# A causal attention stage: value products of two units together, the side products dealt anew, part of q copied by transfers

## The chip, the cores and the metric

The kernel runs on one NeuronCore of a Trainium2 chip. The metric is the device time of one execution in microseconds (us). TensorE (PE) does the matrix products, VectorE (DVE), ScalarE (ACT) and GpSimd (POOL) do the element-wise work, and SyncE (SP) issues most of the DMA transfers. Each engine works through its own instruction stream strictly in the order of the program, and the streams meet only at semaphores: an instruction `wait_ge(s, n)` holds its engine until the counter s has reached n.

## What is computed

One decoder layer on 1024 tokens of width 1024: a pooling mixer and a causal attention with a forget bias side by side, gated and projected; then a cross attention to 256 memory tokens; then a SwiGLU feed-forward layer and a last RMSNorm. The change lies in the causal attention (8 heads of width 64) and in the pooling mixer's output product that runs beside it:

```python
for i in range(S // Q_BLOCK):                       # 8 blocks of 128 queries
    q0, q1 = i * Q_BLOCK, (i + 1) * Q_BLOCK
    s = jnp.einsum('bhqd,bhkd->bhqk', q[:, :, q0:q1], k[:, :, :q1]) * scale
    s = s + c[:, :, q0:q1, None] - c[:, :, None, :q1]   # forget bias
    s = jnp.where(mask[None, None], s, -1e30)
    p = jax.nn.softmax(s, axis=-1)
    outs.append(jnp.einsum('bhqk,bhkd->bhqd', p, v[:, :, :q1]))
y_pool = pool_mixer(u_pool, pool_w, pool_scale) @ w_pool_out
gates = jax.nn.sigmoid(g_logit + b_gate)            # g_pool, g_fox
x = x + (g_pool * y_pool + g_fox * y_fox) @ w_out
```

## The kernel before

The attention is a loop over 32 units, written out once for each engine. Unit u treats the pair of heads p = u // 8 and the query block i = u % 8, so a unit has i + 1 blocks of 128 keys for each of two heads. It is a pipeline over three units:

- PE, scores of unit u (lines 2396 to 2413): two float32r products per head and per 512 keys, into PSUM banks 0 to 3. They wait for `sc_biased` of unit u - 1, because DVE must have read the same banks.
- DVE (lines 1767 to 1777) adds the bias `negc`, finds the minimum (the negated maximum) and writes `prob`. ACT takes the exponential (line 1242), DVE multiplies by the reciprocal of the sum (lines 1785 and 1787) and counts `prob_ready`.
- PE, one unit later: transposes of `prob` (line 2384) in groups of up to four blocks into banks 4 and 5 in turn; ACT copies each group to `prob_t` (line 1233). From the third group on a group waits for the copy that frees its bank.
- PE, two units later: value products `values(u - 2)` (line 2375) into bank 6, with weights of 64 columns, so the array works in two halves of 64 columns. ACT copies the result to `o_sb` (`pv_copy`, line 1215).

So unit u on PE is, in this order: scores(u), values(u - 2), first two groups of transposes(u - 1), side work part 0, the other groups of transposes, side work part 1. In units with i = 0 part 0 stands before the values and part 1 before the later transposes.

Side work (`fill`, line 2327) fills PE's waiting time: the last four products of the stage before (d), eight mixing products (m), and from the twelfth unit on 64 pieces, four for each of 16 output halves v of the pooling mixer's projection. A piece is three products of 512 columns (`mm3`, lines 2172 to 2174), here called a piece. All 16 halves use the same PSUM bank, 7: the first piece of half v waits for `za_done >= v` (line 2356), that is, until DVE has multiplied half v - 1 out of the bank with its gate (`pool_gated`, line 1758). The tables FIRST_FILL and NEXT_FILL (lines 148 to 150) say how many pieces each part of each unit gets, two numbers for a unit. GATED_IN (line 156) derives from them the part in which a half's last piece lies, and DVE's stream has its multiply in that unit: if it is part 0 with i of 4 or more (or 0), behind DVE's bias step of the unit; if it is part 0 with i of 1 to 3, or part 1, behind DVE's multiplies by the reciprocal.

ACT's order in a unit is: the value copy, the copies of the first two groups, the two exponentials, the copies of the other groups, then side jobs. Among these are the splits of the next pair's q and k into a high and a low part (`qk_hi_of`, line 1106). For q each head's scaled half (64 partitions) is written twice by ACT, once into its own partitions and once into the other 64 (lines 1112 and 1114). When a pair is complete, its result is split too (`o_hi_of` on ACT, `o_lo_of` on DVE; units 27 to 29 and behind the loop).

Of the kernel before, what the change touches and what calls it, by code (L numbers as in the profile page):

```python
# [15 lines left out]
FP32 = mybir.dt.float32  # L16
# [6 lines left out]
P = 128  # L23
# [63 lines left out]
LAST = (4, 5, 6, 7, 0, 1, 2, 3)  # L87
PROD2 = 7
# [60 lines left out]
NEXT_FILL = ((0, 2, 1, 1, 2, 2, 1, 2) + (1, 2, 1, 1, 2, 2, 2, 2, 2, 2, 1, 1, 1, 1, 1, 2)  # L149
             + (1, 4, 2, 2, 2, 2, 2, 2, 2, 2, 1, 1, 1, 1, 1, 3))  # L150
# [70 lines left out]
def build(nc, x, mem, norm_mix_g, w_in, b_forget, b_gate, pool_w, pool_scale, w_pool_out,  # L221
# [15 lines left out]
    with ctx:  # L237
# [76 lines left out]
        prob_t = place("prob_t", 136, [P, 2, S])  # L314
        o_sb = place("o_sb", 144, [P, PAIRS, S])
# [90 lines left out]
        pads_zero, win_step, d_ready, d_stored = (sem("pads_zero"), sem("win_step"), sem("d_ready"),  # L406
# [10 lines left out]
        negc_masked, negc_plain = sem("negc_masked"), sem("negc_plain")  # L417
        qk_hi, qk_lo, q2_zeroed, negc_loaded = sem("qk_hi"), sem("qk_lo"), sem("q2_zeroed"), [sem(f"negc_loaded{i}") for i in range(3)]
# [6 lines left out]
        mem_loaded, gain_row_in, ones_set, gain_spread, mix_gain = (sem("mem_loaded"), sem("gain_row_in"), sem("ones_set"),  # L425
# [141 lines left out]
        def _(sp):  # L567
# [88 lines left out]
            def load_qk(p, r):  # L656

                which, h = divmod(r, 2)
                i = r % 2
                if (p, r) in ((2, 0), (2, 1)):  # L660
                    sp.wait_ge(prod_done, N_STAGE + 3)
                if p > 1 or r >= 2:
                    sp.wait_ge(qk_lo, 8 * p + 2 * r - 2 if r >= 2 else 8 * p - 4 + 2 * r + 2)
                else:
                    for s in range(4):
                        sp.wait_ge(c_stored[s], 16 * FST[s, QK_REST[1]])
                    sp.wait_ge(prod_done, N_STAGE)
                sp.dma_start((qk_first if p == 1 else qk_st)[:, i, :], qk_dram[3 * which + p - 1][:, half_of(h)]).then_inc(qk_in[i], 16)
# [388 lines left out]
        def _(act):  # L1057
# [48 lines left out]
            def qk_hi_of(p, r, src, a0=0, a1=2):  # L1106

                which, h = divmod(r, 2)
                for a in range(a0, a1):
                    own, other = slice(a * DH, (a + 1) * DH), slice((1 - a) * DH, (2 - a) * DH)  # L1110
                    if which == 0:
                        nc.scalar.activation(q1[p % 2][a][other, half_of(h)], src[own, :], ACT.Copy,
                                             scale=DH ** -0.5).then_inc(qk_hi, 1)
                    nc.scalar.activation((k1 if which else q1)[p % 2][a][own, half_of(h)], src[own, :], ACT.Copy,
                                         scale=1.0 if which else DH ** -0.5).then_inc(qk_hi, 1)
# [94 lines left out]
            def pv_copy(v):  # L1210
                act.wait_ge(pv_done, v + 1)
                if v == 2 * T:
                    for s in range(4):
                        act.wait_ge(c_stored[s], 16 * FST[s, LAST_PAIR])
                nc.scalar.activation(o_sb[:, v // T, tile_of(v % T)], ps[:, 6, 0:P], ACT.Copy).then_inc(pv_copied, 1)
# [6 lines left out]
            for u in range(PAIRS * T + 1):  # L1222
# [3 lines left out]
                if u >= 2:  # L1226
                    pv_copy(u - 2)
                groups = list(enumerate(groups_of((u - 1) % T))) if u else []

                def copy_groups(part):  # L1230
                    for g, (a, j0, n) in part:
                        act.wait_ge(pt_done, groups_before(u - 1) + g + 1)
                        nc.scalar.activation(prob_t[:, a, j0 * P:(j0 + n) * P], ps[:, 4 + g % 2, 0:n * P],  # L1233
# [23 lines left out]
                if u in (27, 28, 29):  # L1257
                    o_hi_of(u - 27)
# [223 lines left out]
        def _(dve):  # L1482
# [24 lines left out]
            nc.vector.memset(ones_row[:], 1.0).then_inc(ones_set, 1)  # L1507
            dve.wait_ge(consts_set, 6)
            nc.vector.tensor_copy(count[:], count_i[:]).then_inc(pads_zero, 1)
            dve.wait_ge(pads_zero, 1)  # L1510
            nc.vector.reciprocal(inv_count[:], count[:]).then_inc(pads_zero, 1)
# [181 lines left out]
            for n, (g, q) in enumerate(STAGE):  # L1693
                if (g, q) == (U_PAIRS[0], P1):
                    dve.wait_ge(negc_stored, 16)
                    nc.vector.memset(u_sb[:, :, 0:PAD], 0.0).then_inc(pads_zero, 1)
                    for w in win:
                        nc.vector.memset(w[:, 0:PAD], 0.0).then_inc(pads_zero, 1)
                    dve.wait_ge(pads_zero, 5)
# [64 lines left out]
            for u in range(PAIRS * T + 1):  # L1764
# [39 lines left out]
                if u in (27, 28, 29):  # L1804
                    o_lo_of(u - 27)
# [362 lines left out]
        def _(pe):  # L2168
# [88 lines left out]
            pe.wait_ge(ones_set, 1)  # L2257
# [134 lines left out]
            for u in range(PAIRS * T + 1):  # L2392
# [370 lines left out]
```

## Time and profile before

| | us |
|---|---|
| median of 3 runs | 1449.02 (1448.48 to 1449.16) |
| the profiled execution | 1448.73 |
| its span, first to last instruction | 1446.9 |
| PE busy in it | 1421.5 |
| DVE busy | 977.0 |
| ACT busy | 626.9 |
| POOL busy | 559.3 |

The attention runs from about 336 us to 523 us of the span. A row of a timeline gives the start, the duration, the engine, the line, the output and inputs, and how many equal instructions were merged; brackets give the idle time before it and what ended that. A product's duration runs until its last result is written, so products overlap: two of 512 columns follow each other 0.23 us apart although each lasts 0.39 us.

### The profile page before, as it was taken

What the parts mean: (1) busy time and instruction counts of PE and PEld (TensorE: products, weight loads), DVE (VectorE), ACT (ScalarE), POOL (GpSimd) and SP (SyncE); (2) the same over time, 40 slices, a digit from 0 to 9 for tenths busy, and PEclk for the clock granted to TensorE, in tenths of its full rate; (3) what the DMA queues carried; (4) which work ended last, traced back from release to release, by engine and by line L of the source; (5) the groups of instructions that cost most, each with busy time, mean ns of one, the idle gap of its engine ahead of it and who ended that gap; (6) DMA issues with size and microseconds to landing.
All of it is one profiled execution on the core that took longest, in us unless ns stands there. A gap on an engine that the chain in (4) does not pass through costs nothing.

```text
span 1446.9 us, 19339 instructions
## 1 busy us (share of the span) xinstructions
PE 1421.5 (98%) x7065; PEld 1170.8 (81%) x7065; DVE 977.0 (68%) x1393; ACT 626.9 (43%) x1181; POOL 559.3 (39%) x572
## 2 busy tenths in 40 slices
PE   7999999999999999999999999999999999999997
PEld 5778888887678788888888788888888888888886
DVE  7745595646877755327566887777677676795867
ACT  6545343526877642116543533332233222444445
POOL 5743233334555301005011755444444453354402
PEclk9999999999999999999999999999999999999999
DMA  8265263555332145114113213333233334883334
GB/s 212 60 118 124 54 146 80 80 104 181 103 102 91 50 160 203 59 44 145 31 44 117 73 59 110 109 110 109 82 108 109 110 109 183 304 291 97 93 102 146
DMA packets 104952, 166.88 MB, mean 115 GB/s; under 512 B 7278, under 2 KB 63106, under 8 KB 103451
## 3 DMA queue, kind: packets, MB, share of 16 engines
q1 hardware_dynamic: 98072, 145.55, 34.1%
q0 software_dynamic: 3200, 11.57, 2.3%
q10 hardware_dynamic: 3586, 8.52, 1.5%
q8 instruction: 57, 0.93, 0.3%
q14 instruction: 37, 0.30, 0.1%
HBM read 123.32 MB, written 42.30 MB: 114 GB/s over the span
## 4 chain that ended last, share of the span: by engine, by line
PE 89%; ACT 4%; POOL 3%; DVE 2%; issue 1%; DMA 1%; SPq 0%; DVEq 0%; ACTq 0%; POOLq 0%
PE ps L2172 27%; PE ps L2174 27%; PE ps L2173 27%; PE ps L2375 2%; PE ps L2384 2%; ACT prob L1242 1%; ACT prob_t L1233 1%; DMA raw_f<-in_w_in 1%; PE ps L2412 1%; PE ps L2411 1%; PE ps L2179 1%; PE ps L2243 1%; PE ps L2546 0%; POOL tok_f L857 0%; PE ps L2657 0%
## 5 line engine op out<-in xcount | busy, mean ns | idle before, releaser
L2172 PE MATMUL ps<-t_lo,s_hi 128*128 128x512 f32 x308 | 119.9, 389 | 0.1
L2174 PE MATMUL ps<-t_hi,s_lo 128*128 128x512 f32 x308 | 119.8, 389 | 0.0
L2173 PE MATMUL ps<-t_hi,s_hi 128*128 128x512 f32 x308 | 119.8, 389 | 0.0
L2172 PE MATMUL ps<-h_lo_T,w_hi 128*128 128x512 f32 x256 | 100.5, 392 | 1.3 <-ACT u_t L1156 1.0
L1416 ACT ACTIVATE s_hi<-w_raw 128x512 fp32r<-128x512 f32 x77 | 48.7, 632 | 118.0 <-PE ps L2174 91.7
L2174 PE MATMUL ps<-h_hi_T,w_lo 128*128 128x512 f32 x256 | 99.7, 389 | 0.0
L2173 PE MATMUL ps<-h_hi_T,w_hi 128*128 128x512 f32 x256 | 99.6, 389 | 0.0
L1501 DVE TENSOR_TENSOR s_lo<-w_raw,s_hi 128x512 fp32r<-128x512 f32 x77 | 61.1, 793 | 56.3 <-ACT s_hi L1416 56.2
L1432 ACT ACTIVATE p_sb<-ps 128x512 f32<-128x512 f32 x22 | 13.0, 598 | 189.5 <-PE ps L2174 189.5
L2172 PE MATMUL ps<-hf_lo_T,w_hi 128*128 128x512 f32 x212 | 82.5, 389 | 0.0
L2173 PE MATMUL ps<-hf_hi_T,w_hi 128*128 128x512 f32 x212 | 82.5, 389 | 0.0
L2174 PE MATMUL ps<-hf_hi_T,w_lo 128*128 128x512 f32 x212 | 82.5, 389 | 0.0
L2172 PE MATMUL ps<-h_lo_B,w_hi 128*128 128x512 f32 x192 | 76.6, 399 | 3.0 <-DVE h_lo_B L1501 3.0
L2174 PE MATMUL ps<-h_hi_B,w_lo 128*128 128x512 f32 x192 | 75.3, 392 | 0.0
L2173 PE MATMUL ps<-h_hi_B,w_hi 128*128 128x512 f32 x192 | 75.2, 392 | 0.0
L1501 DVE TENSOR_TENSOR w_lo<-s_sum,w_hi 128x512 fp32r<-128x512 f32 x64 | 48.5, 763 | 39.2 <-ACT w_hi L1104 38.8
L964 POOL TENSOR_TENSOR w_sum<-w_raw 128x512 f32<-128x512 f32 x11 | 14.3, 1296 | 156.2 <-DVE w_lo L1501 93.7
L1065 ACT ACTIVATE w_hi<-w_raw 128x1024 fp32r<-128x1024 f32 x32 | 33.9, 1059 | 89.5 <-PE ps L2174 85.9
L2172 PEld LDWEIGHTS ps<-t_lo,s_hi 128*128 128x128 f32 x308 | 57.8, 188 | 12.6 <-issue 0.5
L2174 PEld LDWEIGHTS ps<-t_hi,s_lo 128*128 128x128 f32 x308 | 57.8, 188 | 12.1
L2173 PEld LDWEIGHTS ps<-t_hi,s_hi 128*128 128x128 f32 x308 | 57.8, 188 | 11.9
L2032 DVE TENSOR_TENSOR hq<-ps,p_sb 128x512 f32<-128x512 f32 x11 | 7.6, 690 | 85.6 <-DMA hs_dram<-h_sum 64.6
(380 smaller groups left out, 4320.3 us busy)
## 6 DMA issues: line engine op xcount, KB each, us to landing
w_raw<-hs_dram SPq DMA_DIRECT2D x77, 256.0 KB, 2.7
raw_p<-in_w_ffn_in SPq DMA_DIRECT2D x22, 512.0 KB, 4.6
w_raw<-in_w_ffn_in SPq DMA_DIRECT2D x22, 512.0 KB, 4.3
hs_dram<-h_sum SPq DMA_DIRECT2D x11, 1024.0 KB, 8.9
hs_dram<-hq SPq DMA_DIRECT2D x11, 768.0 KB, 7.0
wq_B<-in_w_ffn_out SPq DMA_DIRECT2D x8, 1024.0 KB, 7.5
raw_f<-in_w_in SPq DMA_DIRECT2D x14, 512.0 KB, 7.3
gate_dram<-c_st SPq DMA_DIRECT2D x28, 256.0 KB, 2.2
```

The lines of the kernel that those rows point to most:

```text
L1065: nc.scalar.activation(w_hi[n % SLOTS][:], w_raw[n % RAWS][:], ACT.Copy).then_inc(hi_ready, 1)
L1233: nc.scalar.activation(prob_t[:, a, j0 * P:(j0 + n) * P], ps[:, 4 + g % 2, 0:n * P], ACT.Copy).then_inc(pt_copied, 1)
L1242: nc.scalar.activation(prob[u % 2][:, a, 0:n], prob[u % 2][:, a, 0:n], ACT.Exp, bias=neg_max[:, u % 2, a:a + 1], scale=-1.0, accum_out=pro ...
L1416: nc.scalar.activation(s2_hi[n % SLOTS2][:], s_raw(n % SLOTS2), ACT.Copy).then_inc(s_split_hi, 1)
L1501: nc.vector.tensor_tensor(out, a, hi.bitcast(FP32), ALU.subtract).then_inc(done, 1)
L2172: nc.tensor.matmul(dst, w_h, x_l, start=start, stop=False, skip_group_check=onto)
L2173: nc.tensor.matmul(dst, w_h, x_h, start=False, stop=False, skip_group_check=onto)
L2174: return nc.tensor.matmul(dst, w_l, x_h, start=False, stop=stop, skip_group_check=onto)
L2179: last = nc.tensor.transpose(two(bank)[:, tile_of(k)], src[:, tile_of(k)], ident[:])
L2243: last = nc.tensor.matmul(ps[0:F_ROWS + HEADS, 5 * h, :], f_w[:, KD * h + 4 * part + j, :], (h_lo if x else h_hi)[ops[part]][:, j, :], sta ...
L2375: last = nc.tensor.matmul(ps[a * DH:(a + 1) * DH, 6, 0:P], v_sb[:, j, hc:hc + DH], prob_t[:, a, tile_of(j)], start=j == 0, stop=j == v % T)
L2384: last = nc.tensor.transpose(ps[:, 4 + g % 2, tile_of(j - j0)], prob[v % 2][:, a, tile_of(j)], ident[:])
```

## The change

- PE does the value products of units 9 to 30 in pairs: none in odd units from 11 on, and in each even unit u from 12 to 32 those of u - 3 and then u - 2 (`values_in`). They use two column blocks of bank 6 in turn, and ACT's two copies stand together. The transposed probabilities of the odd units go to buffers of their own (`odd_t`), in places that others have left; ACT waits in units 10 and 30 for these to be free.
- The pieces of side work of units 12 to 31 are dealt anew (NEXT_FILL). The number of pieces in each couple of an even and the next odd unit stays the same.
- ACT writes only q's own half from the second pair on; two transfers on SP's queue for each half of the columns copy it to the other 64 partitions, at units 3 and 5 of the pair before. The scores of a pair wait for them (`q1_doubled`).
- The results of pairs 0 to 2 are split in units 25 to 27 instead of 27 to 29.
- Two semaphores are merged into one (`dve_set`).

The new table deals the pieces like this (number of half, a point, number of piece; two brackets are part 0 and part 1). Only units in which something differs or a half changes are shown.

```
unit   before                       after
12     [] [0.0 0.1]                 [] [0.0]
13     [0.2] [0.3]                  [0.1 0.2] [0.3]
14     [1.0 1.1] [1.2 1.3]          [1.0] [1.1 1.2]
15     [2.0] [2.1 2.2]              [1.3 2.0] [2.1 2.2]
16     [2.3] [3.0 3.1]              [2.3] [3.0]
17     [3.2] [3.3]                  [3.1 3.2] [3.3]
18     [4.0 4.1] [4.2 4.3]          [4.0 4.1] [4.2]
19     [5.0 5.1] [5.2 5.3]          [4.3 5.0 5.1] [5.2 5.3]
20     [6.0 6.1] [6.2 6.3]          [6.0 6.1] [6.2]
21     [7.0] [7.1]                  [6.3 7.0] [7.1]
22     [7.2] [7.3]                  [] [7.2]
23     [8.0] [8.1 8.2]              [7.3 8.0] [8.1 8.2]
26     [11.0 11.1] [11.2 11.3]      [11.0 11.1] [11.2]
27     [12.0 12.1] [12.2 12.3]      [11.3 12.0 12.1] [12.2 12.3]
28     [13.0 13.1] [13.2 13.3]      [13.0 13.1] [13.2]
29     [14.0] [14.1]                [13.3 14.0] [14.1]
30     [14.2] [14.3]                [] [14.2]
31     [15.0] [15.1 15.2 15.3]      [14.3 15.0] [15.1 15.2 15.3]
```

```diff
@@ -85,6 +85,7 @@
 
 S_AT = (0, 5, 3, 4, 1, 6, 2)
 LAST = (4, 5, 6, 7, 0, 1, 2, 3)
+PAIRED = 9
 PROD2 = 7
 STEPS = PROD2 * NJ
 GROUPS = ((0, 4), (4, 8), (8, 11))
...
@@ -146,8 +147,8 @@
 SPLIT_AT = {5: 0, 7: 1, 12: 2, 18: 3, 23: 4, 28: 5, 32: 6}
 LOW_AFTER = {5: 0, 8: 1, 12: 2, 18: 3, 24: 4, 28: 5}
 FIRST_FILL = (2, 2, 2, 2, 1, 0, 1, 1, 1, 0, 1, 0, 1, 0, 1, 1, 1, 1, 2, 1, 1, 1, 1, 0)
-NEXT_FILL = ((0, 2, 1, 1, 2, 2, 1, 2) + (1, 2, 1, 1, 2, 2, 2, 2, 2, 2, 1, 1, 1, 1, 1, 2)
-             + (1, 4, 2, 2, 2, 2, 2, 2, 2, 2, 1, 1, 1, 1, 1, 3))
+NEXT_FILL = ((0, 1, 2, 1, 1, 2, 2, 2) + (1, 1, 2, 1, 2, 1, 3, 2, 2, 1, 2, 1, 0, 1, 2, 2)
+             + (1, 4, 2, 2, 2, 1, 3, 2, 2, 1, 2, 1, 0, 1, 2, 3))
 DEFER_DONE = {0: 0, 1: 1, 4: 2, 7: 3}
 MIXED_IN = {8: (0, 1), 9: (2, 3), 10: (4, 5, 6), 11: (7,)}
 FILL = [0]
...
@@ -212,6 +213,13 @@
     return q, t, u if u < 8 else 6 + u % 2 if u < 24 else (0, 5)[u % 2]
 
 
+def values_in(u):
+
+    if u < PAIRED + 2:
+        return (u - 2,) if u >= 2 else ()
+    return (u - 3, u - 2) if u % 2 == 0 and u > PAIRED + 2 else ()
+
+
 def unit_count(u):
 
     return FIRST_UNITS.index(u) + 1 if u < 8 else u + 1
...
@@ -312,6 +320,7 @@
         negc = [place(f"negc{i}", kb, [P, S]) for i, kb in enumerate((112, 116, 108))]
         prob = [place(f"prob{i}", 120 + 8 * i, [P, 2, S]) for i in range(2)]
         prob_t = place("prob_t", 136, [P, 2, S])
+        odd_t = {kb: place(f"odd_t{kb}", kb, [P, S]) for kb in (156, 180, 108, 144)}
         o_sb = place("o_sb", 144, [P, PAIRS, S])
 
         gf = [place(f"gf{m}", 4 * m, [P, S]) for m in range(KD)]
...
@@ -485,6 +495,12 @@
 
         def tile_of(t):
             return slice(t * P, (t + 1) * P)
+
+        def turned(v, a):
+
+            if v % 2 == 0 or v < PAIRED:
+                return prob_t[:, a, :]
+            return odd_t[((156, 180), (108, 180), (108, 144))[(v >= 3 * T) + (v >= 29)][a]]
 
         slot_hi = [w_hi[(C_XO + 1 + i // 2) % SLOTS][:, half_of(i % 2)] for i in range(6)] + [t[:, :] for t in late_hi]
         slot_lo = [w_lo[(C_XO + 1 + i // 2) % SLOTS][:, half_of(i % 2)] for i in range(6)] + [t[:, :] for t in late_lo]
...
@@ -665,6 +681,10 @@
                     for s in range(4):
                         sp.wait_ge(c_stored[s], 16 * FST[s, QK_REST[1]])
                     sp.wait_ge(prod_done, N_STAGE)
+                if r >= 2:
+                    for a in range(2):
+                        own, other = slice(a * DH, (a + 1) * DH), slice((1 - a) * DH, (2 - a) * DH)
+                        sp.dma_start(q1[p % 2][a][other, half_of(i)].bitcast(FP32), q1[p % 2][a][own, half_of(i)].bitcast(FP32)).then_inc(q1_doubled, 16)
                 sp.dma_start((qk_first if p == 1 else qk_st)[:, i, :], qk_dram[3 * which + p - 1][:, half_of(h)]).then_inc(qk_in[i], 16)
 
             def load_gate(v):
...
@@ -1108,7 +1128,7 @@
                 which, h = divmod(r, 2)
                 for a in range(a0, a1):
                     own, other = slice(a * DH, (a + 1) * DH), slice((1 - a) * DH, (2 - a) * DH)
-                    if which == 0:
+                    if which == 0 and p == 0:
                         nc.scalar.activation(q1[p % 2][a][other, half_of(h)], src[own, :], ACT.Copy,
                                              scale=DH ** -0.5).then_inc(qk_hi, 1)
                     nc.scalar.activation((k1 if which else q1)[p % 2][a][own, half_of(h)], src[own, :], ACT.Copy,
...
@@ -1208,11 +1228,8 @@
                     front_square(7)
 
             def pv_copy(v):
-                act.wait_ge(pv_done, v + 1)
-                if v == 2 * T:
-                    for s in range(4):
-                        act.wait_ge(c_stored[s], 16 * FST[s, LAST_PAIR])
-                nc.scalar.activation(o_sb[:, v // T, tile_of(v % T)], ps[:, 6, 0:P], ACT.Copy).then_inc(pv_copied, 1)
+                act.wait_ge(pv_done, v + 1 + (v % 2 if PAIRED <= v < PAIRS * T - 2 else 0))
+                nc.scalar.activation(o_sb[:, v // T, tile_of(v % T)], ps[:, 6, tile_of(v % 2)], ACT.Copy).then_inc(pv_copied, 1)
 
             def o_hi_of(p):
                 act.wait_ge(pv_copied, T * (p + 1))
...
@@ -1223,14 +1240,20 @@
                 p, i = divmod(u, T)
                 if u == PAIRS * T:
                     split_hi(SPLIT_AT[u])
-                if u >= 2:
-                    pv_copy(u - 2)
+                for v in values_in(u):
+                    pv_copy(v)
+                if u == PAIRED + 1:
+                    act.wait_ge(def_ev, 4)
+                    for s in range(4):
+                        act.wait_ge(c_stored[s], 16 * FST[s, LAST_PAIR])
+                if u == 30:
+                    act.wait_ge(o_lo_ready, 1)
                 groups = list(enumerate(groups_of((u - 1) % T))) if u else []
 
                 def copy_groups(part):
                     for g, (a, j0, n) in part:
                         act.wait_ge(pt_done, groups_before(u - 1) + g + 1)
-                        nc.scalar.activation(prob_t[:, a, j0 * P:(j0 + n) * P], ps[:, 4 + g % 2, 0:n * P],
+                        nc.scalar.activation(turned(u - 1, a)[:, j0 * P:(j0 + n) * P], ps[:, 4 + g % 2, 0:n * P],
                                              ACT.Copy).then_inc(pt_copied, 1)
 
                 copy_groups(groups[:2])
...
@@ -1254,8 +1277,8 @@
                     qk_hi_of(p + 1, e, (qk_st if p else qk_first)[:, e % 2, :], a0, a1)
                 if u in SPLIT_AT and u < PAIRS * T:
                     split_hi(SPLIT_AT[u])
-                if u in (27, 28, 29):
-                    o_hi_of(u - 27)
+                if u in (25, 26, 27):
+                    o_hi_of(u - 25)
             pv_copy(PAIRS * T - 1)
             o_hi_of(PAIRS - 1)
             for m in (6, 7):
...
@@ -1650,7 +1673,10 @@
             def qk_lo_of(p, r, src, a0=0, a1=2):
 
                 which, h = divmod(r, 2)
-                dve.wait_ge(qk_hi, 12 * p + (4, 8, 10, 12)[r] - (2 if a1 == 1 else 0))
+                if p:
+                    dve.wait_ge(qk_hi, 4 + 8 * p + (2, 4, 6, 8)[r] - (1 if a1 == 1 else 0))
+                else:
+                    dve.wait_ge(qk_hi, (4, 8, 10, 12)[r])
                 for a in range(a0, a1):
                     own, other = slice(a * DH, (a + 1) * DH), slice((1 - a) * DH, (2 - a) * DH)
                     if which:
...
@@ -1801,8 +1827,8 @@
                 if i < 4 and u < 3 * T and i - 1 in SPLIT_HI:
                     e, a0, a1 = SPLIT_HI[i - 1]
                     qk_lo_of(p + 1, e, (qk_st if p else qk_first)[:, e % 2, :], a0, a1)
-                if u in (27, 28, 29):
-                    o_lo_of(u - 27)
+                if u in (25, 26, 27):
+                    o_lo_of(u - 25)
 
             o_lo_of(PAIRS - 1)
             for j in range(4):
...
@@ -2368,17 +2394,17 @@
 
                 pe.wait_ge(pt_copied, groups_before(v + 1))
                 if v:
-                    pe.wait_ge(pv_copied, v)
+                    pe.wait_ge(pv_copied, v - (PAIRED < v and v % 2 == 0))
                 for j in range(v % T + 1):
                     for a in range(2):
                         hc = (2 * (v // T) + a) * DH
-                        last = nc.tensor.matmul(ps[a * DH:(a + 1) * DH, 6, 0:P], v_sb[:, j, hc:hc + DH],
-                                                prob_t[:, a, tile_of(j)], start=j == 0, stop=j == v % T)
+                        last = nc.tensor.matmul(ps[a * DH:(a + 1) * DH, 6, tile_of(v % 2)], v_sb[:, j, hc:hc + DH],
+                                                turned(v, a)[:, tile_of(j)], start=j == 0, stop=j == v % T)
                 last.then_inc(pv_done, 1)
 
             def transposed(v, groups):
                 for g, (a, j0, n) in groups:
-                    if g >= 2:
+                    if groups_before(v) + g >= 2:
                         pe.wait_ge(pt_copied, groups_before(v) + g - 1)
                     for j in range(j0, j0 + n):
                         last = nc.tensor.transpose(ps[:, 4 + g % 2, tile_of(j - j0)], prob[v % 2][:, a, tile_of(j)], ident[:])
...
@@ -2395,6 +2421,8 @@
                 groups = list(enumerate(groups_of(v % T))) if u else []
                 if u < PAIRS * T:
                     pe.wait_ge(qk_lo, 8 * p + 8)
+                    if p:
+                        pe.wait_ge(q1_doubled, 64 * p)
                     if p == 1:
                         pe.wait_ge(q2_zeroed, 4)
                     for a in range(2):
...
@@ -2414,8 +2442,8 @@
                 if u and i == 0 and u < PAIRS * T:
                     beside(u, 0)
                 if u:
-                    if u >= 2:
-                        values(u - 2)
+                    for e in values_in(u):
+                        values(e)
                     pe.wait_ge(prob_ready, 2 * u)
                     transposed(v, groups[:2])
                 if i and u < PAIRS * T:
```

## Rows read from the trace of the kernel before

**Rows 1.** The page's first part: busy time of each engine.
```profile
PE 1421.5 (98%) x7065; PEld 1170.8 (81%) x7065; DVE 977.0 (68%) x1393; ACT 626.9 (43%) x1181; POOL 559.3 (39%) x572
```

**Rows 2.** Timeline of PE, end of unit 18 and unit 19.
```profile
430.80 0.39 PE L2174 MATMUL ps<-d_hi,w_lo 128*128 128x512 f32 x1
...
431.71 0.39 PE L2412 MATMUL ps<-k,q 128*128 128x512 f32 x1
432.02 0.66 PE L2375 MATMUL ps<-prob_t,v_sb 128*64 128x128 f32 x8
432.61 0.88 PE L2384 MATMUL ps<-ident,prob 128*128 128x128 f32 x6
433.25 0.48 PE L2172 MATMUL ps<-d_lo,w_hi 128*128 128x512 f32 x1
```

**Rows 3.** Timeline of PE where transposes follow a piece, unit 22.
```profile
451.29 0.40 PE L2174 MATMUL ps<-d_hi,w_lo 128*128 128x512 f32 x1
451.52 0.82 PE L2384 MATMUL ps<-ident,prob 128*128 128x128 f32 x6
```

**Rows 4.** Waits from 386 to 523 us: engine, line, waited for; total, times, longest.
```profile
PE ps L2375 <- ACT prob_t L1233: 1.7, 5, 0.7
PE ps L2384 <- ACT prob_t L1233: 0.9, 2, 0.7
PE ps L2411 <- DVE neg_max L1775: 0.8, 1, 0.8
```

**Rows 5.** Timelines of DVE and PE: a sum out of bank 7 and the product behind it.
```profile
339.30 0.68 DVE L1738 TENSOR_TENSOR u_t<-ps,u_last 128x512 f32<-128x512 f32 x1
340.13 0.47 PE L2172 MATMUL ps<-h_lo_T,w_hi 128*128 128x512 f32 x1 [0.25 <-DVE u_t L1738]
```

**Rows 6.** Timeline of DVE: units 18 and 19, multiplies out of bank 7.
```profile
431.23 0.69 DVE L1758 TENSOR_TENSOR za<-ps,g_st 128x512 f32<-128x512 f32 x1 [0.48 <-PE ps L2174]
...
435.70 0.62 DVE L1787 TENSOR_SCALAR prob<-prob,prob_inv 128x512 f32<-128x512 f32 x1
436.30 0.69 DVE L1758 TENSOR_TENSOR za<-ps,g_st 128x512 f32<-128x512 f32 x1
```

**Rows 7.** Timeline of DVE, unit 23: two bias steps of 1024 columns.
```profile
455.31 1.22 DVE L1775 CUSTOM_DVE_ANT_0 prob<-ps,negc 128x1024 f32<-128x1024 f32 x1
...
456.45 1.22 DVE L1775 CUSTOM_DVE_ANT_0 prob<-ps,negc 128x1024 f32<-128x1024 f32 x1
```

**Rows 8.** Timelines of PE and DVE, units 22 to 23.
```profile
450.11 0.88 PE L2384 MATMUL ps<-ident,prob 128*128 128x128 f32 x6
...
452.87 0.40 PE L2411 MATMUL ps<-k,q 128*128 128x512 f32 x1
...
454.10 0.69 DVE L1787 TENSOR_SCALAR prob<-prob,prob_inv 128x896 f32<-128x896 f32 x1
454.79 1.53 PE L2375 MATMUL ps<-prob_t,v_sb 128*64 128x128 f32 x24
456.25 0.98 PE L2384 MATMUL ps<-ident,prob 128*128 128x128 f32 x7
```

**Rows 9.** Timelines of PE and DVE, units 20 to 21.
```profile
438.31 1.09 PE L2384 MATMUL ps<-ident,prob 128*128 128x128 f32 x8
441.93 0.55 DVE L1787 TENSOR_SCALAR prob<-prob,prob_inv 128x640 f32<-128x640 f32 x1
442.01 0.39 PE L2411 MATMUL ps<-k,q 128*128 128x512 f32 x1
...
443.48 1.09 PE L2375 MATMUL ps<-prob_t,v_sb 128*64 128x128 f32 x16
```

**Rows 10.** Timeline of DVE, unit 28: the split of a pair's result.
```profile
490.33 2.57 DVE L1501 TENSOR_TENSOR o_lo<-o_sb,o_hi 128x1024 fp32r<-128x1024 f32 x1 [0.54 <-ACT o_hi L1219]
```

**Rows 11.** Timeline of ACT: q's second copy in unit 17.
```profile
426.74 0.63 ACT L1112 ACTIVATE q<-qk_st 64x512 fp32r<-64x512 f32 x1
```

**Rows 12.** The page's DMA issues: KB of each, median us from issue to landing.
```profile
qk_st<-qk_dram SPq DMA_DIRECT2D x8, 256.0 KB, 3.3
```

More of the change, by code:

```diff
@@ L405, in build @@
         f_step, negc_stored, t3_ready = sem("f_step"), sem("negc_stored"), sem("t3_ready")
-        pads_zero, win_step, d_ready, d_stored = (sem("pads_zero"), sem("win_step"), sem("d_ready"),
+        dve_set, win_step, d_ready, d_stored = (sem("dve_set"), sem("win_step"), sem("d_ready"),
                                                            [sem(f"d_stored{i}") for i in range(2)])
@@ L417, in build @@
         negc_masked, negc_plain = sem("negc_masked"), sem("negc_plain")
+        q1_doubled = sem("q1_doubled")
         qk_hi, qk_lo, q2_zeroed, negc_loaded = sem("qk_hi"), sem("qk_lo"), sem("q2_zeroed"), [sem(f"negc_loaded{i}") for i in range(3)]
@@ L423, in build @@
             sem("o_lo_ready"))
-        mem_loaded, gain_row_in, ones_set, gain_spread, mix_gain = (sem("mem_loaded"), sem("gain_row_in"), sem("ones_set"),
+        mem_loaded, gain_row_in, gain_spread, mix_gain = (sem("mem_loaded"), sem("gain_row_in"),
                                                                     sem("gain_spread"), sem("mix_gain"))
@@ L1505, in xt_lo_of @@
                 minus_hi(lo, two(bank).rearrange("p (k n) -> p k n", n=P), hi, xt_lo)
-            nc.vector.memset(ones_row[:], 1.0).then_inc(ones_set, 1)
+            nc.vector.memset(ones_row[:], 1.0).then_inc(dve_set, 1)
             dve.wait_ge(consts_set, 6)
-            nc.vector.tensor_copy(count[:], count_i[:]).then_inc(pads_zero, 1)
-            dve.wait_ge(pads_zero, 1)
-            nc.vector.reciprocal(inv_count[:], count[:]).then_inc(pads_zero, 1)
+            nc.vector.tensor_copy(count[:], count_i[:]).then_inc(dve_set, 1)
+            dve.wait_ge(dve_set, 2)
+            nc.vector.reciprocal(inv_count[:], count[:]).then_inc(dve_set, 1)
             def front_norm(t):
@@ L1695, in _ @@
                     dve.wait_ge(negc_stored, 16)
-                    nc.vector.memset(u_sb[:, :, 0:PAD], 0.0).then_inc(pads_zero, 1)
+                    nc.vector.memset(u_sb[:, :, 0:PAD], 0.0).then_inc(dve_set, 1)
                     for w in win:
-                        nc.vector.memset(w[:, 0:PAD], 0.0).then_inc(pads_zero, 1)
-                    dve.wait_ge(pads_zero, 5)
+                        nc.vector.memset(w[:, 0:PAD], 0.0).then_inc(dve_set, 1)
+                    dve.wait_ge(dve_set, 6)
                 if (g, q) == (QK0[0], P1):
@@ L2256, in _ @@
             pe.wait_ge(gain_row_in, 16)
-            pe.wait_ge(ones_set, 1)
+            pe.wait_ge(dve_set, 1)
             for h in range(2):
```

## The prediction

> **What bounds the kernel now.** I read the page's busy times first. PE works 1421.5 of 1446.9 us [rows 1], so only what PE does or waits for can move the end; DVE and ACT matter where PE waits for them. Then I read the timeline of PE through the attention, about 336 to 523 us, and beside it those of DVE and ACT, to see what follows what and how soon. The view of waits from unit 11 on shows PE waiting 1.7 us in five places for ACT's copies before value products, 0.9 us in two places before transposes, and 0.8 us once for DVE's bias step before scores [rows 4]. The stage is short of slack but PE is nearly full. A gain can come from these 3.4 us and from the gaps between kinds of products; a loss can be as long as anything that PE is newly made to wait for, since no other engine's slack buys back a gap in PE's stream.
>
> **The pairing: gain.** The last score product starts at 431.71 and one of 512 columns takes 0.23 (two neighbours: 451.29 and 451.52 [rows 3]), so the values at 432.02 start 0.08 late. Eight value records take 0.43 (the unit with 24, 454.79 to 456.25, is 0.87 longer for 16 more: 0.054 each [rows 2, 8]), yet the transposes come 0.59 behind: 0.16 late. Transposes straight behind a piece come with no gap [rows 3]. A value block thus costs 0.24 beside its work, and eleven odd units lose theirs: 11 x 0.24 = -2.6 us. The gap is dearer than any other change of kind here. The Trainium skill, TensorEngine Tiling (Array Packing), section Key Properties, says that changing the tiling mode drains the engine; that agrees with a gap only around products with 64-column weights, and with none between two blocks of that kind.
>
> **Waits that go: gain.** The values of the older unit now stand ahead of the younger one's, so ACT's copies for the younger have 1.3 us or more of extra cover in most units. The 1.7 us before values goes whole. Of the 0.9 before transposes, 0.67 is in unit 13, between its only part-0 piece and the later groups; two pieces stand there now. The last 0.25 is in unit 32, where nothing changes. One of the five value waits, 0.67 us, comes from DVE's split of a result, 2.57 us long [rows 10], ahead of a bias step; this moves to units 25 to 27, which have few keys. Together -2.4 us.
>
> **New waits for the softmax: loss.** In an odd unit the transposes now follow the scores at once. From transposes to the next transposes PE must cover copies, exponentials and DVE's multiplies. In unit 22 this chain takes from 450.11 to 454.10 + 0.69 = 454.79, or 4.7 us [rows 8]. PE's cover there will be: twelve transposes at 0.107 each (six take 0.64 [rows 2]), 1.3; the only piece, 3 x 0.23 and 0.08 more for the first product behind transposes (it lasts 0.48 there, not 0.40 [rows 2, 3]), 0.77; scores 1.84 (452.87 to 454.79 less the 0.08); in all 3.9. It stalls 0.8 to 0.9, and in unit 30, dealt alike, too: 1.8. Part of it stands earlier, since an empty part 0 leaves the third group of transposes to wait for ACT, which has two value copies first; that does not change the sum. In unit 12, which keeps one piece, the chain is that of unit 20, 438.31 to 441.93 + 0.55, or 4.2 us, against 0.86 for eight transposes + 0.77 + 1.39 (442.01 to 443.48 less 0.08) = 3.0 [rows 9]: 1.2 us. And unit 9's values leave unit 11, where they stood ahead of the 0.8 us wait for the bias [rows 4] that DVE sets alone: their 0.6 comes on top. In all +3.6 us.
>
> **The new dealing: the large term.** Before, no half of the pooling projection begins in the same part in which the last one ends; scores, values and transposes lie between, and DVE empties bank 7 under them. In the new table units 15, 19, 21, 23, 27, 29 and 31 hold the last piece of one half and, as the very next work, the first of the next. PE must now wait for DVE's multiply out of bank 7, and DVE does that in its own order. All in PE's queue waits behind, the transposes and scores too.
> - The least price, DVE free: the last product starts at 430.80 and the multiply at 431.23, 0.43 later, and takes 0.69 [rows 2, 6]. From DVE's end to PE takes 0.15: a sum out of bank 7 ends at 339.98 and the product behind it starts at 340.13 [rows 5]. Without the wait the next product would start 0.23 on. 0.43 + 0.69 + 0.15 - 0.23 = 1.04 us. I take it for units 21 and 29 and for 15, where DVE's bias step is done in time: 3.1 us.
> - Units 23 and 31 have eight key blocks. The multiply is behind both bias steps, 1.14 us each (455.31 to 456.45 [rows 7]), and those are behind the multiplies of unit 22 or 30, which end as the transposes start. 2 x 1.14 + 0.69 + 0.15 = 3.1 us behind the start of the transposes, where PE arrives after 0.75 (seven transposes) + 0.77 = 1.5. It stalls 1.6 us, twice: 3.2.
> - Units 19 and 27 have i = 3, and there the multiply comes behind the softmax's own multiplies, for which ACT's exponentials must be done. Unit 19 before shows this place in DVE's queue: the transposes start at 432.61, and a multiply out of bank 7, for another half, directly behind the softmax at 436.30 [rows 2, 6]. It ends at 436.99; with 0.15 that is 4.5 us. PE has 0.64 + 0.77 = 1.4 us of work before it needs the bank. It stalls 3.1 us, twice: 6.2.
>
> Sum: 3.1 + 3.2 + 6.2 = +12.5 us. Between 7 x 1.04 = 7.3, if DVE is always free, and about 16, if results' splits and bias steps delay DVE further in units 15, 27 and 29. I take 12.5, since each place in DVE's order is fixed by the program.
>
> **What costs nothing.** ACT loses twelve copies of 0.63 us [rows 11], 7.6 us of work, but in the rows that PE waits for, ACT was itself waiting for PE or DVE, so I give it 0; it could give back at most some tenths in units 9 to 12. The transfers in their place move 128 KB each; one of 256 KB lands 3.3 us after its issue [rows 12], and they are issued at units 3 and 5 of a pair for use in unit 8, over 9 us on. They stand in SP's queue ahead of the loads of k, behind a wait that this load had before; the load starts two issues later and is used more than a unit on. Should they land late, scores of a pair's first unit would wait. ACT's new waits for buffers in units 10 and 30 find them free: the last store there is issued at unit 7, the first split done by unit 26.
>
> **The sum.** -2.6 - 2.4 + 3.6 + 12.5 = +11.1 us. The profiled execution took 1448.7 us, 0.3 under the median of 1449.0, so 1448.7 + 11.1 = 1459.8, and against the median 1460.
>
> **Rivals.**
> - The crossings cost only their least, as DVE reaches each multiply in time: 7.3 in place of 12.5, so 1455. For it: DVE is idle for part of most units (68% busy [rows 1]). Against it: the order of its stream, not its load, sets the moment.
> - Not slower: the handover out of bank 7 hides, and the pairing remains. The sum without it is -2.6 - 2.4 + 3.6 = -1.4, 1447.5, within 0.2%. This decides if seven crossings together cost under 4.3 us, or 0.6 each; the multiply alone lasts 0.69 [rows 6] and can't start before the product is complete. It holds only if I misread which half needs which.
> - Longer stalls let PE's clock fall. The rows show products 0.23 us apart after waits up to 0.8 us [rows 4], thus the 2.4 GHz level; no row here has 3 us of idle time in this stage. If each of the two long stalls were followed by as much time at 1.2 GHz, that would add about 3 us each: 1466. The Trainium skill, TensorE: Matmul & The Clock Gate, section The HAM clock gate, says the clock halves after an idle time; no row here shows it.
> - The change doesn't do what it says: the transfers come too late, and PE waits for q in units 8, 16 and 24. At 1 us each 1463.
>
> **How the numbers follow.** The forecast gets 0.65, the least price 0.17, a fallen clock 0.07, late transfers 0.04, not slower 0.07. The range 1453.5 to 1466 takes in the least price with a little more gain and the upper bound of 16 us with room; it leaves out about 0.15. About 0.2%, 2.9 us, is what a measurement can tell from no change. Faster by more has 0.03, within it 0.05, slower 0.92.
>
> **What would show it.** In the changed trace, line 2172's pieces (first product of a new half) must wait for the multiply into za, about 3 us in units 19 and 27, 1 to 1.6 us in the others: some 12 us under one releaser. Values stand in 12 blocks from unit 12 on (the last, unit 31's, alone), waits of values for `prob_t` are gone, and transposes in units 13, 23 and 31 wait for DVE's multiplies. It is wrong if za's waits are under 7 us in all, or if the clock in those stretches is under 1.0.

## The result

| | kernel before | changed kernel |
|---|---|---|
| median, us | 1448.48 (1448.2 to 1449.16, 5 runs) | 1462.3 (1460.42 to 1463.14, 5 runs) |
| profiled execution, us | 1448.73 | 1460.42 |
| its span, us | 1446.9 | 1458.5 |
| attention stage, us | 176.3 | 189.3 |

The ratio is 1.0091 (95% interval 1.008 to 1.0102): slower by about 13 us. The attention stage is counted here and below from PE's first score product (336.51 before, 336.00 after) to its first product on the low part of the result (512.85 and 525.26). It grew by 12.9 us; all before and behind it is within 1 us of what it was.

The changed kernel's page: PE's work is the same and the span is longer by idle time.

```profile
PE 1422.2 (98%) x7065; PEld 1172.9 (80%) x7065; DVE 976.1 (67%) x1393; ACT 618.7 (42%) x1169; POOL 557.7 (38%) x572
```

Its view of waits, PE from 386 us to the end of the stage (total, times, longest), as in [rows 4]. Ahead of 386 us the waits are those of the kernel before.

```profile
PE ps L2198 <- DVE za L1784: 11.8, 7, 3.3
PE ps L2439 <- DVE neg_max L1801: 1.4, 1, 1.4
PE ps L2410 <- ACT odd_t L1256: 1.2, 3, 0.5
PE ps L2410 <- DVE prob L1813: 0.9, 1, 0.9
```

The first row did not exist before. L2198 is the first product of a piece, L1784 the multiply of a finished half out of bank 7: seven waits, one in each unit where a half ends and the next begins. Four of the seven in PE's timeline, those of units 15, 19, 23 and 27:

```profile
412.69 0.47 PE L2198 MATMUL ps<-d_lo,w_hi 128*128 128x512 f32 x1 [1.02 <-DVE za L1784]
...
436.66 0.47 PE L2198 MATMUL ps<-d_lo,w_hi 128*128 128x512 f32 x1 [3.14 <-DVE za L1784]
...
462.38 0.47 PE L2198 MATMUL ps<-d_lo,w_hi 128*128 128x512 f32 x1 [1.29 <-DVE za L1784]
...
489.08 0.47 PE L2198 MATMUL ps<-d_lo,w_hi 128*128 128x512 f32 x1 [3.28 <-DVE za L1784]
```

and DVE's timeline ahead of the second of them, where the multiply stands directly behind the softmax's own, as at 436.30 before [rows 6]:

```profile
435.43 0.49 DVE L1813 TENSOR_SCALAR prob<-prob,prob_inv 128x512 f32<-128x512 f32 x1
435.83 0.68 DVE L1784 TENSOR_TENSOR za<-ps,g_st 128x512 f32<-128x512 f32 x1
```

DVE ends at 436.51 and PE starts at 436.66: the handover of 0.15 us of [rows 5]. Behind the longest stall PE's clock fell. PE's timeline in unit 27, then the granted clock (the 1.00 or 0.50 behind the busy times) in three windows of 1 us:

```profile
489.85 0.49 PE L2198 MATMUL ps<-d_lo,w_hi 128*128 128x512 f32 x1
490.13 0.63 PE L2199 MATMUL ps<-d_hi,w_hi 128*128 128x512 f32 x1
490.56 0.63 PE L2200 MATMUL ps<-d_hi,w_lo 128*128 128x512 f32 x1
...
493.50 0.39 PE L2439 MATMUL ps<-k,q 128*128 128x512 f32 x1
```

```profile
489.00:490.00 1.00, 0.92 (x4) 0.82 (x5) 0.00 (x0) 0.00 (x0) 0.00 (x0) 1.00 0.03 2
490.00:491.00 1.00, 1.00 (x5) 0.71 (x4) 0.00 (x0) 0.00 (x0) 0.00 (x0) 0.51 0.71 254
491.00:492.00 1.00, 1.00 (x4) 0.81 (x3) 0.00 (x0) 0.00 (x0) 0.00 (x0) 0.50 0.02 6
```

Products are 0.43 us apart from 490.13 on instead of 0.23 [rows 3], the 1.2 GHz level. Eight products pay 0.2 us each: 1.6 us. Behind the other long stall, that of unit 19, the granted clock is 1.00 from 436 to 440 us and the products stay 0.23 apart.

The pairing takes away most of a gap, not all of it. Value blocks in unit 22: x16 from the odd buffer, then x20, then transposes.

```profile
452.56 1.09 PE L2401 MATMUL ps<-odd_t,v_sb 128*64 128x128 f32 x16
453.48 1.26 PE L2401 MATMUL ps<-prob_t,v_sb 128*64 128x128 f32 x20
454.67 0.88 PE L2410 MATMUL ps<-ident,prob 128*128 128x128 f32 x6
...
456.02 0.88 PE L2410 MATMUL ps<-ident,prob 128*128 128x128 f32 x6 [0.47 <-ACT odd_t L1256]
```

The second block starts 0.92 behind the first, where sixteen records take 0.87: a gap of 0.05 between neighbours, against 0.24 around a lone block, so each block that joins another saves 0.19. The last row is the cost of the empty part 0 in this unit: the third group of transposes waits for ACT.

### The profile page after: what moved, and what is told of

It is laid out like the page before. It is cut to its first block, busy times and chain, and to the rows that moved or that the text cites. A ratio compares the mean times of both kernels' runs of the same rounds, so it can differ in the third digit from the quotient of the medians.

```text
span 1458.5 us, 19379 instructions
## 1 busy us (share of the span) xinstructions
PE 1422.2 (98%) x7065; PEld 1172.9 (80%) x7065; DVE 976.1 (67%) x1393; ACT 618.7 (42%) x1169; POOL 557.7 (38%) x572
## 4 chain that ended last, share of the span: by engine, by line
PE 87%; ACT 4%; DVE 3%; POOL 3%; issue 2%; DMA 1%; DVEq 0%; SPq 0%; ACTq 0%; POOLq 0%
PE ps L2198 27%; PE ps L2200 27%; PE ps L2199 27%; PE ps L2401 2%; ACT prob L1265 1%; PE ps L2410 1%; DVE prob L1801 1%; ACT odd_t L1256 1%; DMA raw_f<-in_w_in 1%; PE ps L2205 1%; PE ps L2269 1%; POOL w_lo L831 0%; PE ps L2574 0%; PE ps L2439 0%; PE ps L2440 0%
## 5 line engine op out<-in xcount | busy, mean ns | idle before, releaser
L2198 PE MATMUL ps<-t_lo,s_hi 128*128 128x512 f32 x308 | 119.9, 389 | 0.1
L2198 PE MATMUL ps<-h_lo_T,w_hi 128*128 128x512 f32 x256 | 100.5, 392 | 1.3 <-ACT u_t L1176 1.0
L2198 PE MATMUL ps<-hf_lo_T,w_hi 128*128 128x512 f32 x212 | 82.5, 389 | 0.0
L2198 PE MATMUL ps<-h_lo_B,w_hi 128*128 128x512 f32 x192 | 76.3, 397 | 2.3 <-DVE h_lo_B L1524 2.3
L2198 PEld LDWEIGHTS ps<-t_lo,s_hi 128*128 128x128 f32 x308 | 57.8, 188 | 12.6 <-issue 0.5
L2199 PEld LDWEIGHTS ps<-t_hi,s_hi 128*128 128x128 f32 x308 | 57.8, 188 | 11.8
```

The costliest lines, as they stand in the source:

```text
L2198: nc.tensor.matmul(dst, w_h, x_l, start=start, stop=False, skip_group_check=onto)
L2199: nc.tensor.matmul(dst, w_h, x_h, start=False, stop=False, skip_group_check=onto)
```

## The experiments

All were timed in five rounds beside the kernel before. The stage is that of each profiled execution; lines of code are those of the kernel concerned.

| kernel | median us | ratio to before (95%) | stage us |
|---|---|---|---|
| before | 1448.5 to 1449.4 | 1 | 176.3 |
| changed | 1462.3 | 1.0091 (1.008 to 1.0102) | 189.3 |
| old table | 1445.26 | 0.9972 (0.9962 to 0.9983) | 173.4 |
| before with the new table | 1467.39 | 1.0124 (1.0111 to 1.0138) | 193.5 |
| multiply ahead | 1455.92 | 1.0045 (1.0032 to 1.0058) | 183.7 |
| old table, no pairing | 1446.64 | 0.9981 (0.9972 to 0.999) | 174.5 |
| the same, q copied by ACT | 1448.39 | 0.9992 (0.9983 to 1.0) | 175.3 |
| one crossing, unit 19 | 1450.3 | 1.0007 (0.9999 to 1.0016) | 178.4 |
| one crossing, unit 23 | 1447.05 | 0.9985 (0.9976 to 0.9994) | 174.8 |
| paired from unit 13 | 1445.53 | 0.9974 (0.9964 to 0.9983) | 173.4 |
| the same, k's low part first | 1446.51 | 0.998 (0.9971 to 0.9989) | 174.4 |
| the same as paired from 13, two pieces earlier | 1444.49 | 0.997 (0.9958 to 0.9981) | 171.9 |

**1. The new dealing undone.** Theory: the table alone makes the loss. Rival: the pairing or the transfers do.

```diff
-NEXT_FILL = ((0, 1, 2, 1, 1, 2, 2, 2) + (1, 1, 2, 1, 2, 1, 3, 2, 2, 1, 2, 1, 0, 1, 2, 2)
-             + (1, 4, 2, 2, 2, 1, 3, 2, 2, 1, 2, 1, 0, 1, 2, 3))
+NEXT_FILL = ((0, 2, 1, 1, 2, 2, 1, 2) + (1, 2, 1, 1, 2, 2, 2, 2, 2, 2, 1, 1, 1, 1, 1, 2)
+             + (1, 4, 2, 2, 2, 2, 2, 2, 2, 2, 1, 1, 1, 1, 1, 3))
```

> The changed kernel with the old table of side pieces; pairing, transfers and the early split stay. Theory (the new dealing is the loss): all seven waits of PE for the multiply out of bank 7, 11.8 us in the changed trace, and the stretch at half clock are gone. The pairing gives -2.6, the waits that go -1.8 to -2.4, new waits +1.5 (in unit 13 0.5, in 23 and 31 0.2 each, 0.6 in unit 12): 1445 to 1446.5, 2 to 3.5 us under the kernel before. Rival (the pairing or the transfers cost by themselves): above 1449.

Measured 1445.26, in the expected range and 4.0 us under before by the ratio. The rest of the change is a gain, and the table cost 17 us (1.0091 less 0.9972, of 1449), of which the stages show 15.9. PE's waits from 386 to 520 us:

```profile
PE ps L2439 <- DVE neg_max L1801: 1.4, 1, 1.4
PE ps L2410 <- DVE prob L1813: 0.6, 1, 0.6
PE ps L2439 <- DVE k L1524: 0.5, 2, 0.3
PE ps L2410 <- ACT odd_t L1256: 0.3, 1, 0.3
```

No wait for za is left, where the changed kernel had 11.8 us of them; these rows make 2.8.

**2. The new dealing alone.** The same two lines, changed the other way in the kernel before.

```diff
-NEXT_FILL = ((0, 2, 1, 1, 2, 2, 1, 2) + ...
+NEXT_FILL = ((0, 1, 2, 1, 1, 2, 2, 2) + ...
```

> The kernel before with the new table of side pieces alone. Theory: the seven waits for the multiply out of bank 7 stand here too, 11 to 12.5 us in all, 3.1 each in units 19 and 27, with a fallen clock behind some of them: 1460 to 1463. Rival (the crossings hurt only because the value products have left the odd units, so that here other work covers them): under 1453.

Measured 1467.39, 18 us over before by the ratio and 4 over the expected range: the rival fell, but my price was too low. Two of its seven waits for za, in units 27 and 29:

```profile
491.73 0.47 PE L2172 MATMUL ps<-d_lo,w_hi 128*128 128x512 f32 x1 [2.74 <-DVE za L1758]
...
507.18 0.77 PE L2172 MATMUL ps<-d_lo,w_hi 128*128 128x512 f32 x1 [3.41 <-DVE za L1758]
```

In unit 29 the multiply comes 3.41 us late, not 0.88 as in the changed kernel: here DVE's splits of the results are still in units 27 to 29, ahead of its bias steps. The seven waits make 12.7 us, and against an undisturbed next start each is 0.16 longer: 13.8. The clock fell twice (granted 0.50 from 439 to 442 and from 508 to 510 us, products 0.43 apart), behind waits of 3.05 and 3.41 us and not behind the one of 2.74; by the starts of the products that is 1.6 us each. 13.8 + 3.2 = 17.0 of the 17.2 us by which the stage grew. One thing beside the crossings: the wait of 0.67 us in unit 13 is not in this trace, which has the second piece there and neither pairing nor transfers.

**3. The multiply ahead of the softmax's.** It changes only DVE's order, in units 19 and 27.

```diff
-                if 2 * u in GATED_IN and (i >= 4 or i == 0):
+                if 2 * u in GATED_IN:
                     pool_gated(GATED_IN[2 * u])
...
-                if 2 * u in GATED_IN and 0 < i < 4:
-                    pool_gated(GATED_IN[2 * u])
```

> The changed kernel, but DVE's multiply out of bank 7 stands ahead of the softmax's multiplies in units 19 and 27 too, as it does in the units with four or more key blocks. Theory (the place in DVE's order sets the wait): the waits in units 19 and 27 fall from 3.1 and 3.3 us to about 1.0 each, 4.4 us less, and with no stall near 3 us left the clock doesn't fall, which gives 1.7 us for each fall: 1454.5 to 1457, and runs that lie closer together than the 1460.4 to 1463.1 of the changed kernel. Rival (ACT or the exponentials set the wait): within 1 us of the changed kernel, 1461 to 1463.

Measured 1455.92 (1454.87 to 1456.46), in the range. DVE's and PE's timelines in unit 19 and the total:

```profile
433.66 0.69 DVE L1784 TENSOR_TENSOR za<-ps,g_st 128x512 f32<-128x512 f32 x1 [0.24 <-PE ps L2198]
```

```profile
434.50 0.47 PE L2196 MATMUL ps<-d_lo,w_hi 128*128 128x512 f32 x1 [0.88 <-DVE za L1784]
```

```profile
PE ps L2196 <- DVE za L1784: 7.8, 7, 1.5
```

The waits fell by 4.0 us (to 0.88 in unit 19 and 1.51 in unit 27) and the granted clock is 1.00 throughout the stage; the stage is 5.6 shorter, 4.0 and the 1.6 of the fallen clock. So it is DVE's order that made these two waits long. The runs lie 1.6 us apart instead of 2.7, which is too little to say that the spread came from the clock.

**4. Neither table nor pairing.** PAIRED = 31, the old table, and ACT's wait for free buffers left in unit 10.

```diff
-PAIRED = 9
+PAIRED = 31
...
-                if u == PAIRED + 1:
+                if u == 10:
```

> The changed kernel with the old table and without the pairing (each unit has the values of two units back, as before): what is left is q's second copy by transfers and the early split of the results. Theory: the early split gives back the 0.67 us wait in unit 30 and some tenths around it, the transfers give 0 to 0.3: 1447.3 to 1448.2, 0.5 to 1.2 under the kernel before. Rival (the transfers delay something, or ACT's relief was worth more): over 1448.5, or under 1447.

Measured 1446.64, 2.7 us under before by the ratio and on the side of the rival (under 1447): more than I expected of transfers and early split. The stage is 1.9 shorter. The pairing thus gives 1.1 us of stage; the ratios say 1.3, but their intervals overlap. PE's waits from 386 us on are 2.0 us here and 2.8 with the pairing (experiment 1), so the gaps gave 1.9 and new waits took 0.8 of it. I had given 2.6 for the gaps: 0.24 for each of eleven blocks, where the runs show 0.17 (1.9 over eleven), since two value blocks side by side still have 0.05 between them.

**5. q copied by ACT again.** As 4, without the transfers and their waits, and ACT's second copy in every pair.

```diff
-                    if which == 0 and p == 0:
+                    if which == 0:
...
-                        sp.dma_start(q1[p % 2][a][other, half_of(i)].bitcast(FP32), ...).then_inc(q1_doubled, 16)
-                        pe.wait_ge(q1_doubled, 64 * p)
```

> The kernel with the old table and without pairing, and ACT makes q's second copy again: only the early split of the results is left of the change. Against the kernel before, the stage should gain the 0.7 to 1.1 us around unit 30 and keep the 0.67 us wait in unit 13: 1447.5 to 1448.3. If the transfers gave nothing, it equals the version with transfers, 1446.6.

Measured 1448.39, 0.1 over the expected range and 1.2 under before by the ratio; 0.9992 against 0.9981 makes 1.6 us for the transfers, with intervals that overlap. In its trace PE waits in unit 13 as in the kernel before:

```profile
402.08 0.77 PE L2403 MATMUL ps<-ident,prob 128*128 128x128 f32 x5 [0.66 <-ACT prob_t L1252]
```

This wait isn't in the trace of 4. The stages differ by 0.8 us, which is this wait and one of 0.17 before the transposes of unit 11. Another 0.6 lies behind PE's last product: see the end.

**6. One crossing, in unit 19.** The old table, one piece later.

```diff
-NEXT_FILL = (... + (1, 2, 1, 1, 2, 2, 2, 2, 2, 2, 1, 1, ...
+NEXT_FILL = (... + (1, 2, 1, 1, 2, 1, 3, 2, 2, 2, 1, 1, ...
```

> The changed kernel with the old table, in which one piece alone moves from unit 18 to unit 19, so that half 4 ends and half 5 begins in part 0 of unit 19. Theory (a crossing costs what DVE's order makes PE wait, and nothing hides it): one wait of about 3.1 us for the multiply out of bank 7 and the same total later, 3 us over the 1445.3 of the kernel without the crossing, thus 1448 to 1448.6; if the clock falls behind the wait, as once in the changed kernel, 1450. Rival (waits that stand anyway later in the stage absorb a part): under 1447.

Measured 1450.3, 5.0 us over the kernel without it by the ratios (1.0007 and 0.9972), and its stage is 5.1 longer. One wait of 3.14 us, then the clock (windows of 1 us, columns as above):

```profile
436.03 0.57 PE L2198 MATMUL ps<-d_lo,w_hi 128*128 128x512 f32 x1 [3.14 <-DVE za L1784]
```

```profile
437.00:438.00 1.00, 1.00 (x4) 0.81 (x3) 0.00 (x0) 0.00 (x0) 0.84 (x4) 0.50 0.40 133
438.00:439.00 1.00, 1.00 (x4) 0.71 (x4) 0.00 (x0) 0.00 (x0) 0.39 (x1) 0.50 0.00 0
```

3.3 for the crossing (from the last product's start to the next, less 0.23) and 1.6 for the clock, together 4.9 of the 5.1. Nothing absorbs it. Moving one piece of 0.7 us by one unit costs 5 us.

**7. One crossing, in unit 23.** As 6, with the piece moved from unit 22 to 23.

```diff
-... 2, 2, 1, 1, 1, 1, 1, 2)
+... 2, 2, 1, 1, 1, 0, 2, 2)
```

> The changed kernel with the old table, one piece moved from unit 22 to unit 23, so that half 7 ends and half 8 begins in part 0 of unit 23. Theory: one wait of 1.3 us for the multiply out of bank 7, 1.5 us against the undisturbed next start, as in the changed kernel; some 0.5 us more before the transposes of unit 22, which lost a covering piece; no stretch at half clock, since no stall is near 3 us. Attention stage 2.0 us longer than the 173.4 of the old table, time 1447.3 against 1445.3. Rival (any crossing pulls the clock down): 1449.

Measured 1447.05, 1.9 over the old table by the ratios; the stage is 1.5 longer.

```profile
453.91 0.98 PE L2410 MATMUL ps<-ident,prob 128*128 128x128 f32 x7 [0.65 <-DVE prob L1813]
...
456.89 0.47 PE L2198 MATMUL ps<-d_lo,w_hi 128*128 128x512 f32 x1 [1.30 <-DVE za L1784]
```

Both waits came as expected and the clock stayed up. The stage grew by less than their sum of 2.1, in part since the scores of unit 24 no longer meet the wait for k's low part (0.34 us in 1).

**8. Pairing from unit 13.** As 1, with PAIRED = 13.

```diff
-PAIRED = 9
+PAIRED = 13
```

> The old table, pairing from unit 13 on instead of 9. The values of units 9 to 12 return to their places: the wait of unit 12 for the bias falls from 1.42 to 0.87 us and the 0.61 before the transposes of unit 12 goes, which is 1.2 less, while two blocks more cost 0.5: 1444.6, 0.7 under the version paired from 9 on (1445.3). Rival (the early pairs pay for themselves): 1445.3 or more.

Measured 1445.53, ratio 0.9974 against 0.9972: no gain, as the rival had it.

```profile
392.12 0.47 PE L2439 MATMUL ps<-k,q 128*128 128x512 f32 x1 [0.87 <-DVE neg_max L1801]
...
415.68 0.33 PE L2439 MATMUL ps<-k,q 128*128 128x128 f32 x1 [0.49 <-DVE k L1524]
```

The waits in units 12 and 13 went as expected (1.42 to 0.87, and 0.61 to none). PE then came to unit 16 earlier and met a longer wait for k's low part, 0.49 for 0.15. The two value blocks more, 0.5 by the expectation, take another part of the gain.

**9. k's low part first.** As 8, in units 7, 15 and 23.

```diff
+                if i == 7 and u < 3 * T:
+                    e, a0, a1 = SPLIT_HI[6]
+                    qk_lo_of(p + 1, e, (qk_st if p else qk_first)[:, e % 2, :], a0, a1)
                 for a in range(2 if u < PAIRS * T else 0):
...
-                if i >= 4 and u < 3 * T and i - 1 in SPLIT_HI:
+                if 4 <= i < 7 and u < 3 * T and i - 1 in SPLIT_HI:
```

> As the one paired from unit 13 on, and DVE makes the low part of k ahead of the bias step in units 7, 15 and 23. The waits of the scores of units 8, 16 and 24 for it, 1.07, 0.15 and 0.34 us in the trace of the version with the old table, go; in unit 8 some 0.6 may come back before the values, as the exponentials of unit 7 are later: 1 us under the one without it, 1443.6. Rival (the later bias step is on the path of its own unit): the same or slower, 1444.6 to 1446.

Measured 1446.51, 1 us slower than 8 and 0.5 over the range of the rival, whose side it is on.

```profile
372.11 0.33 PE L2442 MATMUL ps<-k,q 128*128 128x128 f32 x1 [0.53 <-DVE neg_max L1804]
...
374.25 1.75 PE L2404 MATMUL ps<-prob_t,v_sb 128*64 128x128 f32 x28 [0.79 <-ACT prob_t L1256]
...
459.73 0.33 PE L2442 MATMUL ps<-k,q 128*128 128x128 f32 x1 [0.65 <-DVE neg_max L1804]
```

The same scores also need the bias step, which was now the later one: a wait changed its name. In unit 8 it became shorter (0.53 for 1.06), but a new one of 0.79 stands before the values, and in unit 24 it doubled.

**10. Two pieces earlier.** As 8; work goes ahead of the waiting scores, and still no half begins in the part in which one ends.

```diff
-NEXT_FILL = ((0, 2, 1, 1, 2, 2, 1, 2) + (1, 2, ..., 1, 1, 1, 1, 1, 2)
-             + (1, 4, 2, 2, ...
+NEXT_FILL = ((0, 2, 1, 1, 2, 2, 1, 3) + (0, 2, ..., 1, 1, 1, 1, 1, 3)
+             + (0, 4, 2, 2, ...
```

> The version paired from unit 13 on, with one piece moved from unit 16 to the end of unit 15 and one from unit 24 to the end of unit 23, so that each stands ahead of the scores that wait 0.49 and 0.32 us for the low part of k. If nothing else is late, these waits go: 0.8 us under that version, 1444.7 against 1445.5, and 4.5 us under the kernel before. Rival (the scores of unit 16 and 24 then come later and their softmax is missed one unit on): no gain.

Measured 1444.49 (1444.7 expected), the best of all; its interval overlaps that of 8. The stage is 1.5 us shorter than in 8, more than the 0.8 of the two waits: a wait of 0.49 in the view is 0.66 us of delay (414.79 + 0.23 to 415.68 in 8), so the two are 1.1 of the 1.5. From unit 12 on these are its only waits over 0.2 us:

```profile
391.92 0.47 PE L2439 MATMUL ps<-k,q 128*128 128x512 f32 x1 [0.87 <-DVE neg_max L1801]
...
508.45 1.14 PE L2410 MATMUL ps<-ident,prob 128*128 128x128 f32 x8 [0.25 <-ACT odd_t L1256]
```

## Why the prediction was right

It said 1460, range 1453.5 to 1466; 1462.3 was measured. The large term and its cause are right. That the sum came so near (11.1 us against 12.9 of stage) is partly luck, since the smaller terms missed in both directions. By the idle times of the two profiled executions, and for the gaps by experiments 1 and 4, the terms are 12.9 for the dealing, 1.6 for the clock, 2.6 for new waits, -2.5 for waits that go and -1.9 for the gaps, 12.7 in all. By its own steps:

- **The dealing, +12.5.** Right, with its places and nearly its sizes. Against an undisturbed next start the waits are 1.18, 1.04 and 1.05 in units 15, 21 and 29 (1.04 forecast), 1.46 and 1.45 in 23 and 31 (1.6), 3.31 and 3.45 in 19 and 27 (3.1): 12.9 in all. Experiments 1, 2 and 6 show the cause, 3 that DVE's order sets the two long ones.
- **The pairing, -2.6.** Right in kind, too large: experiments 1 and 4 give 1.9 for the gaps. The sum took the whole 0.24 of a lone block as saved and forgot what stays between neighbours, 0.05.
- **The waits that go, -2.4.** Right: no value product waits from unit 12 on (1.7 us), and the 0.67 of unit 13 is gone, with 0.17 before the transposes of unit 11 that I had not counted. I put the 0.67 down to the second piece in part 0 of unit 13. That piece is enough, as 2 shows, but so are the transfers, as 4 shows with the old table; in 5, with neither, the wait is back.
- **ACT's relief, 0.** Wrong for the old table: there the transfers gave 0.8 us of stage, nearly all in units 12 and 13, where ACT was behind, and I had allowed "some tenths". In the changed kernel the larger part of this, the wait of unit 13, was already counted above.
- **New waits for the softmax, +3.6.** Too large: 2.6. Unit 12's wait grew from 0.79 to 1.42, as forecast; before unit 12's transposes PE waits 0.94 (1.2 forecast). In units 22 and 30 I had 0.9 each for DVE's multiplies. PE waits 0.47 and 0.53 there, at the third group of transposes and for ACT's copies, and the transposes of the next units, 23 and 31, do not wait at all.
- **The fallen clock.** I had it as a rival with 0.07, for both long stalls together, and named a clock under 1.0 in these stretches as a sign of being wrong. The sign came: the clock fell behind one of the two in the profiled execution, for 1.6 us, and behind single stalls in 2 and 6. It should have been a term of the sum. Its price in the prediction was wrong too: 3 us at half the clock lose 1.5 us, not 3. Whether the longer runs of the changed kernel, up to 1463.1, had a second fall is open: their traces were not kept, and the mean granted clock is 0.997 in the runs of 1460.4, 1462.3 and 1462.9 us and 0.994 in that of 1463.1. A spread of this size can also come from ahead of the stage: its first score starts between 336.0 and 338.1 us in the twelve profiled executions.
- **The rival of least prices (1455)** is nearly what experiment 3 made on purpose: 1455.9. **Late transfers** did not occur: no scores wait for q.

## What to carry to other kernels

When filler work is dealt to slots by count, it has its own dependences: where one result ends and the next begins in the same buffer, put other work between, or the filler is what stalls the engine. The size of such a stall is read from where the release stands in the other engine's order, not from how busy that engine is. And a wait that is taken away often uncovers the next one: 1.2 us of waits removed in experiment 8 gave nothing, partly because the next wait grew by 0.3, and the gain came when work was put ahead of that one.

## What the runs showed of the hardware

- Four stalls of PE, of 3.05 and 3.41 us in experiment 2, 3.28 in the changed kernel and 3.14 in experiment 6, were followed by products at 0.43 us instead of 0.23, which cost 1.6 us each time. But one of 3.14 in unit 19 of the changed kernel was not, nor one of 2.74 in experiment 2, nor any of up to 1.5 us in the stage. The Trainium skill, TensorE: Matmul & The Clock Gate, section The HAM clock gate, says that the clock halves after idle time; the granted clock of 0.50 in two of the windows above agrees, and the wait of unit 19 shows that idle time of this length need not do it.
- In all nine profiled kernels with the transfers of q the span ends 933.2 to 933.4 us behind the end of the stage, in the three without them 933.9 to 934.1. PE's own timeline behind the stage is equal to 0.1 us; the 0.6 us lie behind the last store's issue. Why is open.
